# A third place for prepared weights at both post-norms of block 1, three loads open together, masks stored as bytes

## The reference

```python
x = x + rmsnorm(merged @ w_out[l], g_post_mix[l])
h = rmsnorm(x, g_pre_ffn[l])
u = causal_dwconv(h @ w_up[l], ffn_conv_w[l], ffn_conv_b[l])
a, g = jnp.split(u, 2, axis=-1)
f = (jax.nn.gelu(a) * g) @ w_down[l]
x = x + rmsnorm(f, g_post_ffn[l])
```

```python
h = rmsnorm_2(x, norm_mix[layer])
hq, hf, hi, hg, sq, sk, sv, iq, ik, iw, mq = split_in(h @ w_in[layer])
# indexer of the sparse attention, for each block of 128 queries
s = jnp.einsum('bqhd,bsd->bqhs', iqb.astype(f32), ik32)
score = jnp.einsum('bqh,bqhs->bqs', iwb, jax.nn.relu(s))
```

## Time and profile before

| | |
|---|---|
| time, median of 3 runs | 1634.99 us (1633.8 to 1635.36) |
| the profiled execution | 1635.36 us, of which span 1633.6 us |
| PE busy | 1567.8 us, 96% of the span |
| DVE busy | 901.2 us, 55% |
| ACT busy | 627.0 us, 38% |
| POOL busy | 11.8 us, 1% |
| loads moved | 150.18 MB, mean 92 GB/s |

### The profile page before, as it was taken

How to read it: one execution, slowest core, us unless ns; L and a number is a source line. 1 busy time by engine, 2 the same in 40 slices (tenths; PEclk the granted TensorE clock), 3 DMA queues, 4 the chain that set the end, 5 groups by cost and what they waited for, 6 DMA issues and landing times.

```text
span 1633.6 us, 20708 instructions
## 1 busy us (share of the span) xinstructions
PE 1567.8 (96%) x7842; PEld 1311.6 (80%) x7842; DVE 901.2 (55%) x1441; ACT 627.0 (38%) x862; POOL 11.8 (1%) x16
## 2 busy tenths in 40 slices
PE   5999999999999899999999889998989999999999
PEld 5888787888877688888888767998878788888887
DVE  4443465544553877776532857978965444434322
ACT  5451434332233444444332535564463323232211
POOL 0000000000000000000000000000000000000000
PEclk9999999999999899999999999999999999999999
DMA  8312221222222122222322312202002222222222
GB/s 291 125 77 103 75 75 52 103 85 95 103 83 97 52 103 92 90 101 103 129 103 103 118 52 77 78 26 74 31 27 89 92 103 101 81 101 103 103 103 77
DMA packets 25705, 150.18 MB, mean 92 GB/s; under 512 B 2563, under 2 KB 4995, under 8 KB 9260
## 3 DMA queue, kind: packets, MB, share of 16 engines
q1 hardware_dynamic: 25644, 149.35, 26.1%
HBM read 147.21 MB, written 2.13 MB: 91 GB/s over the span
## 4 chain that ended last, share of the span: by engine, by line
PE 83%; DVE 9%; ACT 4%; issue 2%; SPq 1%; DMA 1%; DVEq 0%; ACTq 0%
PE bank L1676 25%; PE bank L1678 25%; PE bank L1677 25%; ACT w_hi L569 2%; PE bank L1790 2%; PE bank L2074 1%; PE bank L1770 1%; DVE w_lo L1033 1%; PE bank L2011 1%; DVE sel L1452 1%; DVE st L1451 1%; DMA raw<-weights 1%; PE bank L1779 1%; DVE w_lo L1041 1%; DVE mx L1163 0%
## 5 line engine op out<-in xcount | busy, mean ns | idle before, releaser
L1676 PE MATMUL bank<-h_hi,w_hi 128*128 128x512 f32 (+1 forms) x1200 | 475.7, 396 | 12.6 <-DVE h_lo L1106 9.9
L1033 DVE TENSOR_TENSOR w_lo<-raw,w_hi 128x2048 fp32r<-128x2048 f32 x118 | 270.3, 2291 | 369.3 <-ACT w_hi L569 368.9
L1678 PE MATMUL bank<-h_hi,w_lo 128*128 128x512 f32 (+1 forms) x1200 | 469.2, 391 | 0.0
L1677 PE MATMUL bank<-h_lo,w_hi 128*128 128x512 f32 (+1 forms) x1200 | 468.9, 391 | 0.0
L569 ACT ACTIVATE w_hi<-raw 128x2048 fp32r<-128x2048 f32 x128 | 244.5, 1910 | 345.7 <-PE bank L1678 342.5
L1676 PEld LDWEIGHTS bank<-h_hi,w_hi 128*128 128x128 f32 (+1 forms) x1200 | 225.5, 188 | 67.6 <-DVE h_lo L1106 9.4
L1678 PEld LDWEIGHTS bank<-h_hi,w_lo 128*128 128x128 f32 (+1 forms) x1200 | 225.5, 188 | 48.7
L1677 PEld LDWEIGHTS bank<-h_lo,w_hi 128*128 128x128 f32 (+1 forms) x1200 | 225.7, 188 | 47.3 <-issue 0.9
L1676 PE MATMUL bank<-a_hi,w_hi 128*128 128x512 f32 x352 | 136.9, 389 | 0.0
L1677 PE MATMUL bank<-a_lo,w_hi 128*128 128x512 f32 x352 | 136.9, 389 | 0.0
L1678 PE MATMUL bank<-a_hi,w_lo 128*128 128x512 f32 x352 | 136.9, 389 | 0.0
(11 more groups left out here) (283 smaller groups left out, 1913.1 us busy)
## 6 DMA issues: line engine op xcount, KB each, us to landing
raw<-weights SPq DMA_DIRECT2D x128, 1024.0 KB, 4.8
toep<-bias_scratch SPq DMA_DIRECT2D x8, 448.0 KB, 4.4
x<-xT SPq DMA_DIRECT2D x1, 2048.0 KB, 18.0
x_tok<-x_tok SPq DMA_DIRECT2D x1, 2048.0 KB, 15.9
outT<-x SPq DMA_DIRECT2D x8, 256.0 KB, 4.2
memT<-memT SPq DMA_DIRECT2D x2, 512.0 KB, 5.9
raw<-weights SPq DMA_DIRECT2D x2, 512.0 KB, 7.6
mem_tok<-mem_tok SPq DMA_DIRECT2D x1, 1024.0 KB, 12.7
```

The costliest lines, as they stand in the source:

```text
L1033: nc.vector.tensor_tensor(w_lo[m % 2][:, :], raw[m % 2][:, :], w_hi[m % 2][:, :].bitcast(F32), ALU.subtract).then_inc(lo_ready, 1)
L1676: nc.tensor.matmul(o, lh, rh, start=first, stop=False)
L1677: nc.tensor.matmul(o, lh, rl, start=False, stop=False)
L1678: return nc.tensor.matmul(o, ll, rh, start=False, stop=last)
```

## The change

Four pairs of buffers stand in place of two. `w_hi[2]`, `w_lo[2]` and `w_hi[3]`, `w_lo[3]` lie in memory that is free at the two post-norms. A table `PLACE` says which pair a load uses. Load `up + 1` uses pair 2 and load `iq` pair 3; all others alternate between 0 and 1. `raw` stays at two buffers.

At the first norm, `up`, `up + 1` and `up + 2` are open together with lags 0, 0 and 5 slices: steps 0 to 4 have 12 matmuls, 5 to 7 have 18, 8 to 12 have 6. The sum stays behind step 7, and the spread comes after step 10. Load `up + 1` is now rounded and split while `w_out` still runs. A second feed-forward turn is written out (`up_second`, banks 0 to 3), and the loop has nine turns in banks 4 to 7.

At the second norm, `iq`, `iq + 1` and `idx` are open with lags 0, 3 and 6: steps 0 to 2 have 6 matmuls, 3 to 5 have 12, 6 and 7 have 18, 8 to 10 have 12, 11 to 13 have 6. The spread comes after step 9. The sum and spread of the post-norm itself move into the middle of the first two `mem_kv_2` tiles. The rounding of `iq + 1` moves behind slice 2 and its split behind residual tile 3; the split of `idx` moves from behind the norm to behind residual tile 5.

The masks come as bytes, 7 levels instead of 8, with no conversion on POOL. `sel` is no longer zeroed: the first of eight heads writes it instead of adding. `aT` is no longer zeroed: its diagonal is written by a multiplication with the identity (`keep_diagonal`) in place of a predicated copy. At block 2's feed-forward norm the new `together` gives the same order as before.

```diff
+PLACE, PREVIOUS = [], []
+_shift = 0
+for _m in range(NLOADS):
+    if _m in (FIRST["up"] + 1, FIRST["iq"]):
+        PLACE.append(2 + _shift)
+        PREVIOUS.append(FIRST["w_out" if _shift == 0 else "mem_kv_2"] - 1)
+        _shift = 1 - _shift
+        continue
+    PLACE.append((_m + _shift) % 2)
+    PREVIOUS.append(max([_n for _n in range(_m) if PLACE[_n] == PLACE[_m]], default=None))
...
-    loop("up", [0, 1, 2, 3], FT // 2 - 1, {1: FIRST["up"] + 2, 3: FIRST["up"] + 3}, 2)
+    tiles("up_second", 4, first=FIRST["up"] + 2, per=2)
+    loop("up", [4, 5, 6, 7], FT // 2 - 2, {1: FIRST["up"] + 4, 3: FIRST["up"] + 5}, 2)
...
-            sp.dma_start(masks_in[:, :, :], A["masks"]).then_inc(mask_in, 16)
+            sp.dma_start(masks[:, :, :], A["masks"]).then_inc(mask_in, 16)
...
-            nc.gpsimd.tensor_copy(masks[:, :, :], masks_in[:, :, :]).then_inc(set_up, 1)
-            nc.gpsimd.memset(sel[:, :, :], 0.0).then_inc(set_up, 1)
-            nc.gpsimd.memset(aT[:, :, :], 0.0).then_inc(set_up, 1)
...
@@ scalar
-                    if m >= 2:
-                        act.wait_ge(w_used, m - 1)
+                    if PREVIOUS[m] is not None:
+                        act.wait_ge(w_used, PREVIOUS[m] + 1)
...
                 round_w(FIRST["w_out"] + m + 1)
+                if m == 3:
+                    round_w(FIRST["up"] + 1)
...
             norm_root("mix", S)
-            round_w(FIRST["up"] + 1)
+            round_w(FIRST["up"] + 2)
             for j in range(KT):
                 next_input("g_pre_ffn", j)
-            round_w(FIRST["up"] + 2)
             norm_root("ffn", S)
+            round_w(FIRST["up"] + 3)
             keep_rms("ffn", rms)
...
@@ vector
             norm_scale("ffn", S)
-            split_w(FIRST["up"] + 2)
+            split_w(FIRST["up"] + 3)
...
-            def up_turn(name, i=None):
-                it = 0 if i is None else i + 1
+            def up_turn(name, it, i=None):
                 for m in range(2):
                     if i is not None:
-                        split_w(FIRST["up"] + m + 4, i, 2)
-                    elif m:
-                        split_w(FIRST["up"] + 3)
+                        split_w(FIRST["up"] + m + 6, i, 2)
+                    elif it + m == 1:
+                        split_w(FIRST["up"] + it + 4)
...
                 if j == 0:
                     split_w(FIRST["iq"])
-                if j == 2:
+                if j == 3:
                     split_w(FIRST["iq"] + 1)
+                if j == 5:
+                    split_w(FIRST["idx"])
...
@@ tensor
+            together("ffn", LOW_END["merged"],
+                     [two_tiles(0, FIRST["up"], "up_first", 0), two_tiles(0, FIRST["up"] + 1, "up_first", 2),
+                      two_tiles(5, FIRST["up"] + 2, "up_second", 0)], KT + 2)
+            weights(FIRST["up"] + 3)
+            for c in range(2):
+                claim(("up_second", 2 + c))
+                done(("up_second", 2 + c), feature_tile(B(("up_second", 2 + c)), FIRST["up"] + 3, c, *H))
...
+            together("x_2", LOW_END["mem_2"],
+                     [two_tiles(0, FIRST["iq"], "iq", 0), two_tiles(3, FIRST["iq"] + 1, "iq", 2),
+                      (6, FIRST["idx"], [(("ik", 0), 0, P), (("iwT", 0), P, P + IDXH)])], KT + 1)
```

More of the change, by code:

```diff
@@ L278, in build @@
         rms = at("rms", AR + 96 * K, [S])
+        for s in range(2):
+            w_hi.append(at(f"w_hi{2 + s}", AR + (40 - 40 * s) * K, [SLOT], F32R))
+            w_lo.append(at(f"w_lo{2 + s}", AR + (48 - 40 * s) * K, [SLOT], F32R))
         br_hi = at("br_hi", AR, [3 * 4, S], F32R)
@@ L799, in up_turn @@
                                          ).then_inc(a_up, 1)
-            up_turn("up_first")
-            with act.Fori(0, FT // 2 - 1) as i:
-                up_turn("up", i)
+            up_turn("up_first", 0)
+            up_turn("up_second", 1)
+            with act.Fori(0, FT // 2 - 2) as i:
+                up_turn("up", i + 2, i)
             act.wait_ge(mem2_in, 16)
@@ L822, in _ @@
             round_w(FIRST["iq"])
-            next_input("norm_mix_2", 0)
+            for j in range(3):
+                next_input("norm_mix_2", j)
             round_w(FIRST["iq"] + 1)
-            for j in range(1, 3):
-                next_input("norm_mix_2", j)
             act.wait_ge(rms_col, 3)
@@ L1361, in up_turn @@
                                             ).then_inc(a_down, 1)
-            up_turn("up_first")
-            with dve.Fori(0, FT // 2 - 1) as i:
+            up_turn("up_first", 0)
+            up_turn("up_second", 1)
+            with dve.Fori(0, FT // 2 - 2) as i:
                 link.enter(i, 4)
-                up_turn("up", i)
-            link.leave(FT // 2 - 1)
+                up_turn("up", i + 2, i)
+            link.leave(FT // 2 - 2)
             dve.wait_ge(a_down, FT + 2)
@@ L1393, in _ @@
             dve.wait_ge(w_used, FIRST["mem_kv_2"] + 2)
-            residual("down", out_tile, "g_post_ffn", "norm_mix_2", range(4, KT))
+            residual("down", out_tile, "g_post_ffn", "norm_mix_2", range(4, KT), between)
             norm_scale("x_2", S, keep=0)
-            split_w(FIRST["idx"])
             def head_norm(src, sq, tokens, keep=None):
@@ L1523, in _ @@
                     for h in range(HG):
-                        keep(h, LEVELS, ("self", h))
+                        keep_diagonal(h)
                     for h in range(HG):
@@ L1700, in token_tile @@
                                   kt == 0, kt == KT - 1)
+                    if inside is not None:
+                        inside(kt)
                 return ins
@@ L1731, in norm_spread, with together @@
                                                         start=True, stop=True))
-            def together(name, first, fresh, norm_name):
-                lag = 3
-                for step in range(KT + lag):
-                    for load in range(2):
-                        kt = step - lag * load
+            def together(norm_name, fresh, loads, spread_step):
+                for step in range(KT + loads[-1][0]):
+                    for lag, ld, tiles_ in loads:
+                        kt = step - lag
                         if not 0 <= kt < KT:
@@ L1987, in turn_heads @@
                 turns(name, 2, lambda f, t: src[:, t, f * P:(f + 1) * P], tokens // P)
-            ld = FIRST["idx"]
-            weights(ld)
-            claim(("ik", 0))
-            done(("ik", 0), feature_tile(B(("ik", 0)), ld, 0, *H))
-            claim(("iwT", 0))
-            for kt in range(KT):
-                ins = product(B(("iwT", 0))[0:IDXH, :], w(ld, 1)[:, kt, P:P + IDXH], w(ld, 0)[:, kt, P:P + IDXH],
-                              h_hi[:, kt, :], h_lo[:, kt, :], kt == 0, kt == KT - 1)
-            done(("iwT", 0), ins)
             claim(("iw", 0))
```

110 lines of the change are left out of this document (55 added, 55 removed).

## The result

The changed kernel takes 1642.76 us (median of 6 runs, 1639.66 to 1645.22) against 1635.2 us of the kernel before (6 runs, 1633.8 to 1635.36). The ratio is 1.0043, with a 95% interval from 1.0033 to 1.0053: 7.6 us slower, where 5.2 us were forecast. The profiled execution of after took 1645.22 us (span 1643.4 us), the slowest of its six, so its trace holds more loss than the median does.

The account below looks back on a forecast made before the run. PE was taken as the bound (83% of the span), losing time by waits and low clock. First norm +6.5, second norm -0.8, sel -0.4, diagonal -0.1 gave +5.2 us: median 1640.2 us, range 1635.2 to 1644.2 us.

Parts of the forecast that it names:

- the claim of bank 2 behind the spread: First norm: PE needs bank 2 for up_second tile 2 before DVE has read it, and stands still 8.7 us.
- The size of the first norm: Whole first norm, later claim plus half clock behind the wait: +6.5 us, between +4.4 and +9.8 us.
- 3.7 us: First norm: low clock assumed from PE's start on h at 537.3 us to 541.0 us, ends 3 and 6.9 us.
- The slow stretch behind the wait: First norm, behind the bank 2 wait: PE restarts at half clock, a loss of 1.7 us, between 1.5 and 3.5 us.
- The loop behind: Feed-forward loop after the first norm: no further wait builds up and it costs nothing, with a margin of 0.3 us.
- The third rival: Feed-forward loop falls behind too, with upper ends of the clock terms: +10.9 us, 1645.9 us, chance 0.10.
- the second: Rival: loss and gain nearly cancel, second norm at its best end of -2.8 us: +0.7 us, 1635.7 us, chance 0.12.
- The four waits: Second norm: PE waits 1.4, 1.2, 2.4 and 0.8 us for slices, 5.8 in place of 4.8 us.
- The net of -0.8 us: Second norm: earlier sum and residual against longer slice waits, -0.8 us taken, ends -2.8 and +1.5 us.
- the 0.4 us of the forecast: Indexer: three of 24 additions into sel become products with one operand less, on which PE waits; 0.4 us saved.
- The rival "the bank wait is not there": First norm: DVE reads tile 2 by 573.1 us, PE keeps a 3.9 us lead; 1629.8 us, chance 0.08.
- The other terms of its sum, -1.3 us: Outside the first norm: second norm -0.8 us, additions into sel -0.4 us, diagonal copies -0.1 us.

Follow-up runs that it names:

- e1: The changed kernel with tiles 2 and 3 of up_second in banks 4 and 5, the loop in 2, 3, 6, 7: 1632.68 us, ratio 0.9987.
- e2: The changed kernel with DVE reading tiles 2 and 3 ahead of the split in the feed-forward turn, banks unchanged: 1634.89 us, ratio 1.0003.
- e4: The changed kernel with its first norm undone; second norm, masks, sel and diagonal as changed: 1634.32 us, ratio 0.9995.
- e3: The changed kernel with the edits of both e1 and e2: 1629.96 us, ratio 0.997.
- e8: The changed kernel with the first norm's sum and spread moved forward, behind slices 5 and 6: 1638.91 us, ratio 1.0026.
- e7: e3 with the idx load no longer opened at the second norm but behind the two iq loads: 1630.8 us, ratio 0.9965.
- e9: e7 with e8's earlier sum and spread at the first norm added: 1629.65 us, ratio 0.9964.
- e5: The kernel before with only the masks part: byte masks, no fills, first head written, diagonal by one multiply: 1634.19 us, ratio 0.9996.

## Why the prediction was right, point by point

**Direction and mechanism: right, and shown.** The forecast named the claim of bank 2 behind the spread. After has the spread at 569.96 us (forecast 569.9), PE's last matmul ahead of the wait at 573.36 us (PE was to be through at 573.1), and the claim passed at 581.89 us (581.8). That these clock times agree to 0.1 us is luck: PE started on `h` 0.9 us earlier than forecast and needed 0.9 us more from there to the spread (33.53 us for 32.6). The time from spread to claim is 11.93 us, what it was before, and that is no luck: DVE's and ACT's steps between are the same. The wait was put at 8.7 us, and the profile has 8.14 us beside what remained of the last matmul. That it is the claim, and not the third load as such, is shown by e1 and e2. In e1 the extra turn claims no bank that waits for the second read, and the kernel is faster than before; e2 moves only that read forward and is level.

**The size of the first norm was too small:** +6.5 forecast, +7.77 in the traces, and by the medians 7.6 + 0.4 = 8.0 us (after against before, plus the 0.4 us by which e4 is faster, whose interval holds a ratio of 1). Two terms of the sum make the 1.3 us. From the first matmul on `h` to the claim PE took 581.89 - 536.43 = 45.46 us in place of 44.5: the low clock lasted 5.3 to 5.6 us where 3.7 us were taken from the end of the second norm's stretch. The row of the first norm itself, 6.9 us, would have been too long, but was nearer. The 3 us at the second norm were only what was left of a stretch that had begun before the wait: in before the clock is down from 923.4 to 930.3 us, 6.9 us, with the wait of 2.74 us inside. In the same way the clock at the first norm of after is down 8.2 us ahead of the first matmul on `h`, so how much of it PE meets there is not set by how dense the start is alone. Windows of before at the second norm, and of after ahead of `h`:

```profile
923.40:930.30 6.90, 4.16 (x10) 2.57 (x9) 6.83 (x10) 3.59 (x8) 0.00 (x0) 0.51 0.43 152
```

```profile
528.25:536.43 8.18, 2.59 (x5) 0.99 (x6) 6.22 (x12) 3.47 (x5) 0.00 (x0) 0.50 0.24 71
```

The slow stretch behind the wait and the loop then cost 7.77 - 5.76 = 2.0 us in place of 1.7.

The rule of the Trainium skill, page "TensorE: Matmul & The Clock Gate", section "Loop structure matters more than you think", has the trace's support in one half. Behind a wait of 8.14 us the clock was 0.50 for 4.2 us, and behind one of 3.41 us it was 0.53 for 3.6 us. But a start without gaps did not set the length of the low clock: with the same unbroken matmuls it lasted from 3.1 to 6.0 us in seven kernels, so a dense start does not by itself end the low clock early here.

**The loop behind: right.** The split that the forecast put at 612.9 us starts at 612.42, and the one ahead of it waits 8.70 us for ACT's rounding, which waits for PE, as forecast. PE has no further wait. The third rival did not occur, and neither did the second: the second norm gave none of the 2.8 us that it needed. In e1 PE is further ahead, and the next claim does cost it 1.41 us; with the second read forward as well (e3) it costs nothing.

**The second norm: the waits nearly right, the net not shown.** The four waits were put at 1.4, 1.2, 2.4 and 0.8 us and measured 1.47, 0.99, 3.19 and 0.28, in sum 5.93 for 5.8. The root step took 0.17 us as forecast, and `diag` and the weights no longer hold PE. The net of -0.8 us is 0.0 in the trace of after, and +0.3 us in e4's; e1, e2 and e3 have 0.0 too, and e8, with the same program there, +0.7. The return of the clock behind the long wait moves this stretch by 1.1 us between executions of the same code, so that neither -0.8 nor zero is shown. e3 against e7 finds no difference in time. What the third load is worth there stays open, below what these runs resolve.

**The indexer and the rest: the saving did not reach PE.** The first heads' operations (mean of each shape in ns, the second number behind the bar) are now

```profile
L1453 DVE TENSOR_SCALAR sel<-relu,iw 128x512 f32<-128x512 f32 x1 | 0.5, 487 | 0.1
L1453 DVE TENSOR_SCALAR sel<-relu,iw 128x384 f32<-128x384 f32 x1 | 0.4, 419 | 0.1
L1453 DVE TENSOR_SCALAR sel<-relu,iw 128x256 f32<-128x256 f32 x1 | 0.4, 353 | 0.7 <-ACT relu L875 0.7
```

for 754, 618 and 484 ns: 0.6 us less on DVE. From the `iwT` transposes to `hf` the traces give -1.0 to -1.2 us in six kernels, -0.2 and -0.3 us in e8 and e9, and +0.4 us in after. That looks like more than the forecast 0.4 us, but the clock accounts for all of it. The windows from the indexer's first matmul to `hf`, of before, after, e1 and e8:

```profile
965.73:983.54 17.81, 17.81 (x49) 10.92 (x49) 14.08 (x23) 10.87 (x24) 0.00 (x0) 0.85 0.18 60
972.62:990.81 18.19, 18.19 (x48) 11.17 (x49) 13.53 (x23) 11.06 (x24) 0.00 (x0) 0.83 0.17 59
961.86:978.67 16.81, 16.81 (x48) 10.24 (x49) 13.21 (x23) 10.95 (x24) 0.00 (x0) 0.90 0.18 64
971.38:988.96 17.58, 17.58 (x49) 10.76 (x49) 13.54 (x23) 11.05 (x24) 0.00 (x0) 0.86 0.18 61
```

PE has no gap in any of them. Read in steps of 0.5 us, the half clock lasts 5.5 us in before, 6.2 in after, 3.0 to 3.4 in the six and 4.9 to 5.0 in e8 and e9, and half of each difference gives the change of the stretch to within 0.1 us. So the shorter products on DVE saved PE nothing that these traces show, and the 0.4 us of the forecast has no support; e5's median is 0.7 us lower without excluding none.

**The rival "the bank wait is not there"** did not hold for this kernel, but its price was good. It put PE's lead at 3.9 us and the time at 1629.8 us. Once the wait was removed (e3, e7, e9) the lead was 2.5 to 3.6 us, and the medians 1629.65 to 1630.8. The other terms of its sum, -1.3 us, are not seen in the traces, so part of that agreement is luck.

The Trainium skill, page "Perfetto Trace Analysis", section "Optimizing Tensor Performance", says that independent groups of matmuls should go round through different banks, so that one is read while the next is computed. The change does use new banks for the loop, but sends tiles 2 and 3 of its extra turn to banks 2 and 3, whose tiles are read last. The runs agree with the rule: 1632.68 us with other banks, 1642.76 us without. In e1 the banks taken hold tiles too; what counts is that those are read 9.4 us earlier (569.61 and 579.02 us).

## What to carry to other kernels

When PE is given more work ahead of a norm's scale, the scale comes later by that work, and so does every read of a bank; count the matmuls that are left between the spread and the first claim of a bank that still holds a tile, and set them against the time from the spread to that read. Give the extra tiles banks that are free or are read first, and put a reader's next read ahead of weight preparation that nothing needs yet. If a step is to be moved forward, look for what stands ahead of its consumer in that engine's queue: a spread 8.0 us earlier brought 1.9 us, with a rounding that waited for PE, and the split that waited for the rounding, in front. And price a stretch of low clock from where the clock falls, not from the next matmul.

## What the runs showed of the hardware that was not expected

The low clock at the start on `h` lasted 3.1, 3.1, 3.5, 5.5, 5.6, 6.0 and 6.0 us in seven kernels with the same gap-free matmuls behind the same wait of 3.4 us: 1.5 us of difference in the span without any in the program. In all seven the granted clock had gone to 0.50 already 6.9 to 8.3 us ahead of that matmul, where PE had only the few matmuls of the sum and the spread, with waits between them. Counted from there, the half clock lasted 10.2 us in e1, e2 and e9 and 13.7 us in after, e3, e7 and e8. Behind the wait of 3.41 us in e2, PE's first 0.8 us were at a granted clock of 1.00 and only the next 3.6 us at 0.53, so that the fall came after the restart. And in the profiled execution of after the clock was at the half level for most of 7.2 us, behind a wait of 1.38 us; in the kernel before the same wait left it at 1.00.
